# A hybrid-attention decoder trunk: the spread of the attention gate row behind the first output tile, and four adaLN sums six to three steps earlier

## The reference

```
mod = silu(c) @ w_ada[l] + b_ada[l]                 # six rows: sh1 sc1 gt1 sh2 sc2 gt2
h = x * (1 + sc1) + sh1
y = concat(rms_norm(window_attention(h)), rms_norm(sparse_attention(h))) @ w_o
x = layer_norm(ALPHA * x + (1 + gt1) * y)
h = x * (1 + sc2) + sh2
x = layer_norm(ALPHA * x + (1 + gt2) * swiglu(h))
```

## Time and profile before

| what | value |
|---|---|
| median of 3 runs | 1323.13 us (1321.76 to 1323.23) |
| the profiled execution | 1322.47 us, span 1320.7 us |
| TensorE matmul busy (PE) | 1256.3 us, 95% |
| VectorE busy (DVE) | 816.4 us, 62% |
| ScalarE busy (ACT) | 510.0 us, 39% |
| GpSimd busy (POOL) | 267.5 us, 20% |
| mean granted TensorE clock | 0.991 |

### The profile page before, as it was taken

The page is one execution under the profiler, slowest core; times in us unless marked ns, Lnnn a source line. Parts: engine busy times, 40 slices in busy tenths (PEclk is TensorE's granted clock), DMA queues, the critical chain, the costliest instruction groups (busy, mean ns, idle before and its releaser), DMA issues.

```text
span 1320.7 us, 18346 instructions
## 1 busy us (share of the span) xinstructions
PE 1256.3 (95%) x6368; PEld 1041.9 (79%) x6368; DVE 816.4 (62%) x1430; ACT 510.0 (39%) x1016; POOL 267.5 (20%) x258
## 2 busy tenths in 40 slices
PE   3999998999999999999999999899999999999996
PEld 3787776788888878888879687788888878888884
DVE  6779999656767765333675678955643345433337
ACT  3444557516333212222244556771543321222210
POOL 4116226800111100000006246671000000000001
PEclk9899999999999999999999999999999999999999
DMA  9563102231777735222424210012132233222211
GB/s 357 186 225 112 65 33 97 92 132 66 255 268 258 253 108 208 96 95 97 160 83 139 65 64 1 33 49 97 64 112 95 95 112 128 96 96 95 95 48 64
DMA packets 44849, 158.29 MB, mean 120 GB/s; under 512 B 5872, under 2 KB 5872, under 8 KB 44784
## 3 DMA queue, kind: packets, MB, share of 16 engines
q1 hardware_dynamic: 30528, 109.07, 24.0%
q0 software_dynamic: 12960, 47.19, 10.7%
q10 hardware_dynamic: 1296, 1.17, 0.3%
HBM read 155.31 MB, written 2.10 MB: 119 GB/s over the span
## 4 chain that ended last, share of the span: by engine, by line
PE 78%; DVE 13%; issue 4%; ACT 3%; POOL 1%; DMA 1%; DVEq 0%; ACTq 0%; POOLq 0%
PE bank L605 23%; PE bank L607 23%; PE bank L606 23%; DVE scores L1573 2%; PE bank L909 2%; PE bank L876 2%; DVE top L1565 2%; DVE w_lo L1423 2%; PE bank L855 1%; PE bank L887 1%; DVE pq L1612 1%; DVE ada_acc L1469 1%; PE bank L637 1%; ACT scratch L1180 1%; POOL w_raw L484 1%
## 5 line engine op out<-in xcount | busy, mean ns | idle before, releaser
L605 PE MATMUL bank<-hT_hi,w_hi 128*128 128x512 f32 (+1 forms) x768 | 286.3, 373 | 2.0 <-issue 1.5
L607 PE MATMUL bank<-hT_hi,w_lo 128*128 128x512 f32 (+1 forms) x768 | 285.3, 371 | 0.0
L606 PE MATMUL bank<-hT_lo,w_hi 128*128 128x512 f32 (+1 forms) x768 | 285.2, 371 | 0.0
L1829 DVE TENSOR_TENSOR w_lo<-w_raw,w_hi 128x1024 fp32r<-128x1024 f32 x88 | 107.8, 1225 | 149.8 <-ACT w_hi L1319 149.8
L1165 ACT ACTIVATE w_hi<-w_raw 128x1024 fp32r<-128x1024 f32 x96 | 100.5, 1062 | 208.7 <-PE bank L607 200.9
L605 PE MATMUL bank<-w_hi,hT_hi 128*128 128x512 f32 (+2 forms) x448 | 170.8, 381 | 4.1 <-ACT pq L1201 2.0
L605 PEld LDWEIGHTS bank<-hT_hi,w_hi 128*128 128x128 f32 x768 | 144.7, 188 | 28.0 <-issue 2.2
L606 PE MATMUL bank<-w_lo,hT_hi 128*128 128x512 f32 (+2 forms) x448 | 164.9, 368 | 0.0
L607 PE MATMUL bank<-w_hi,hT_lo 128*128 128x512 f32 (+2 forms) x448 | 164.7, 368 | 0.0
L607 PEld LDWEIGHTS bank<-hT_hi,w_lo 128*128 128x128 f32 x768 | 144.6, 188 | 25.3
L606 PEld LDWEIGHTS bank<-hT_lo,w_hi 128*128 128x128 f32 x768 | 144.7, 188 | 24.6
(11 more groups left out here) (172 smaller groups left out, 1878.2 us busy)
## 6 DMA issues: line engine op xcount, KB each, us to landing
w_raw<-in_weights SPq DMA_DIRECT2D x184, 512.0 KB, 3.5
ada_w<-in_w_ada POOLq DMA_DIRECT2D x80, 512.0 KB, 4.9
ada_w<-in_w_ada SPq DMA_DIRECT2D x4, 512.0 KB, 6.5
qT<-in_w_ada SPq DMA_DIRECT2D x4, 512.0 KB, 10.1
xs<-in_x SPq DMA_DIRECT2D x4, 512.0 KB, 15.6
g_row<-in_ln_row POOLq DMA_DIRECT2D x4, 512.0 KB, 5.5
b_row<-in_ln_row POOLq DMA_DIRECT2D x4, 512.0 KB, 6.8
trunk_out<-xs SPq DMA_DIRECT2D x8, 256.0 KB, 2.1
```

The source lines that it names most:

```text
L605: pe.matmul(dst, a_hi, b_hi, start=first, stop=False)
L606: pe.matmul(dst, a_hi, b_lo, start=False, stop=False)
L607: return pe.matmul(dst, a_lo, b_hi, start=False, stop=last)
L1829: nc.vector.tensor_tensor(w_lo[:, s, :], w_raw[:, s, :], w_hi[:, s, :].bitcast(F32), ALU.subtract).then_inc(lo_ready, 1)
```

## The change

In layer 0's attention the last four adaLN sums, and GpSimd's four fetches that go with them, move from steps 64, 65, 66, 67 to 58, 60, 62, 64. In both layers `spread_gate` moves behind `out_first` of tile 3, with its own waits. Nothing is added or removed.

```diff
-ASIDE_AT = (12, 18, 24, 30, 42, 46, 50, 54, 64, 65, 66, 67)
+ASIDE_AT = (12, 18, 24, 30, 42, 46, 50, 54, 58, 60, 62, 64)
...
                     if 0 <= i - LAG_V < 64:
                         head_values(l, (i - LAG_V) // 8, (i - LAG_V) % 8)
+                    if i - 64 - LAG_V in (0, 1):
+                        out_first(l, WO0_ORDER[i - 64 - LAG_V])
                     if i == 64 + LAG_V:
 
                         pe.wait_ge(masked, at_head(l, 7, 7))
                         spread_gate(l, 0, 4)
-                    if i - 64 - LAG_V in (0, 1):
-                        out_first(l, WO0_ORDER[i - 64 - LAG_V])
```

## The result

The change made the kernel slower by a quarter of a percent: 1324.62 us median of 20 runs, against 1322.10 for the kernel before, ratio 1.0023 with a 95% interval of 1.0013 to 1.0032, which is +3.0 us (+1.7 to +4.2); the means of the two sets are 3.0 us apart, the medians 2.5. The profiled execution took 1326.54 us, span 1324.8 us. Single runs spread over 6 us for either kernel, so a comparison of two whole traces says little about a change of this size: of the 4.1 us between the two spans, 2.25 had come about before the first moved instruction. I therefore read the stage from an anchor inside each trace: from the start of GpSimd's fourth low half (line 492, just ahead of the first difference) to TensorE's first product of the adaLN reduction behind tile 2 (line 629). I call this **the interval**.

The account below looks back on a forecast made before the run. Bound: GpSimd's late root for unit 6, delaying ScalarE's copies and TensorE's last products. Layer 0 +1.0, layer 1 +0.1 and clock +1.3 gave +2.4 us on the 1323.13 median: 1325.5 us, 8-in-10 range 1322.9 to 1327.6.

Parts of the forecast that it names:

- Fetches: GpSimd, layer 0: three fetches of 0.63 us each now stand ahead of unit 6's root, +1.9 us on the chain.
- Sums beside gains: Layer 0: GpSimd gains slowed by VectorE sums running beside them, +0.5 us, bounds 0 and 2.9.
- d = 2.4 us: Predicted delay of unit 6's root on GpSimd in layer 0: 1.9 for fetches plus 0.5 for sums beside gains.
- The removed wait: Layer 0, TensorE ahead of tile 3: its wait for the last adaLN sum before the spread goes, -1.4 us.
- The clock: TensorE, layer 0: idle growing to 3.2 us drops the next stretch to 1.2 GHz, +1.3 us, bounds 0 and 2.0.
- Layer 1: No sum is pending there; tile 3 now waits briefly for its low half, +0.1 us.
- Covers: VectorE's step 58 sum, late masks, late root ask and late gate take all stay hidden, price nothing.
- the line that I had drawn at 0.2%: Smallest difference from no change that a measurement of this kernel was said to tell: about 0.2%, 2.6 us.
- the clock holds: Rival, chance 0.25: neither TensorE stretch around the idle is empty enough to lower the clock; +1.1, 1324.2 us.
- GpSimd's delay is absorbed: Rival, chance 0.08: unit 6's root has hidden slack, so only the removed wait counts; 1321.8 us.
- the blocked case: Rival, chance 0.15: sums 60, 62 and 64 each take 0.9 to 1.0 us from a GpSimd gain half; 1327.8 us.
- low-clock stretch in layer 1: Rival, chance 0.10: the shift makes such a stretch come or go, 1.4 us either way; 1322.8 to 1326.9 us.

Follow-up runs that it names:

- fetches late: The change with GpSimd's four fetches put back at steps 64 to 67, sums left early; 1322.70 us, ratio 0.9994 to the kernel before.
- Short sum: The change with the sum of step 60 over only 64 of its 1024 columns; 1323.23 us, one run.
- spread only: The kernel before with only the spread moved, sums and fetches left at steps 64 to 67; 1321.87 us, ratio 0.9980.
- filled wait: The change with eight unused products in TensorE's idle ahead of the last head's transpose, layer 0; 1323.90 us, ratio 1.0002 to the kernel before.
- change, root first: The change with GpSimd's gains of steps 60 and 62 moved to 62 and 63, behind unit 6's root; 1322.29 us, ratio 0.9986 to before.

## Why the prediction was right, step by step

- **What bounds the stage.** Right: after 252.90 the root's delay passes through one to one. The root is 2.94 us later behind the anchor, TensorE's idle 2.95 us longer.
- **Fetches, +1.9 us.** Right. The three take 0.63, 0.58 and 0.58 us, and from each to the row behind it 0.68, 0.62 and 0.60, 1.9 in all; "fetches late" takes 2.2 us off the root, this and some of the contention, whose pattern shifts with it.
- **Sums beside gains, +0.5 us.** This is the term that was mis-sized. I had placed the gain of step 58 0.1 us ahead of sum 60 and so counted it as undisturbed. They started within 0.02 us of each other, the gain lost 1.08 us, and the second pair 0.1: +1.1 to 1.2 in all, inside the bounds of 0 and 2.9. "Short sum" shows that the sum was the cause. An order worked out to 0.1 us from the trace of before was not enough to choose between the two ends of the bound.
- **d = 2.4 us** was thereby 2.94, and layer 0 without the clock +1.5 instead of +1.0.
- **The removed wait, -1.4 us.** Nearly: "spread only" took 1.56 us off the interval.
- **The clock, +1.3 us.** Right: it fell, and cost 2.93 - 1.54 = 1.4 by the intervals (1.55 with the 1.56 of "spread only" in place of 1.4), 1.5 by the filled wait.
- **Layer 1, +0.1.** Right, 0.09. There the spread's move never gains, since no sum is pending.
- **Covers.** The sum of step 58, the late masks and ask, and the late take of the gate all stayed hidden, with 3.0 us left ahead of unit 7's low half in both layers.
- **Sum.** +2.4 forecast, +3.0 measured, by the intervals as by the timed runs. The 0.6 us is the contention term. The measured 0.23% lies just over the line that I had drawn at 0.2%, with an interval (0.13 to 0.32%) that reaches to both sides of it; but it excludes no change at all, so these runs told a change of 0.1% from none, and not only one of 0.2%. That the median of 1324.62 is only 0.9 us below the forecast of 1325.5 is partly luck: the forecast started from 1323.13, the median of three runs, and twenty runs gave 1322.10.
- **The rivals.** The case in which the clock holds and the one in which GpSimd's delay is absorbed did not occur. Of the blocked case about a third did: one sum of three, that of step 60, took 1.1 us from a gain, and this was a sign that I had named for it. By the condition that I gave there, slower from d = 2.7 with a fall of the clock, the measured d of 2.94 falls on its side. The low-clock stretch in layer 1 did move, from 785.5 to about 849.7 in the profiled executions, with the 1.18 us named above; what it is worth in the timed runs is not shown.

I had priced "the wait removed" against both parts of the change together. The runs show that either part removes it alone, so that the parts don't add: the spread's move is worth 1.56 us alone and nothing behind early sums.

## What to carry to other kernels

When a wait for a side task is to be removed, move the consumer behind independent work before moving the producer: the spread's move alone took 1.6 us off, while the producer's move brought a queue of another engine with it. Count, on every queue, each instruction that a shared step table moves ahead of a critical one, here three fetches of 0.6 us ahead of a root that others waited for. And look first at what stands ahead of a late small instruction: putting the root ahead of gains that nothing waited for yet gave 0.9 us for two changed table entries.

## What the runs showed of the hardware

- A gain of GpSimd, which reads SBUF, that starts while a VectorE sum with two inputs in SBUF runs ends late by nearly the rest of that sum: 1.08 us beside a sum that started at the same time and took 1.28, 0.48 beside one that had 0.6 us left. This agrees with the exclusive lock in the Trainium skill (SBUF — State Buffer, Who interferes with whom). A sum that starts inside a gain lost about 0.3 us (two took 2.86 instead of 2.54), less than that rule gives.
- Even an operation on one column is held up: GpSimd's root took 1.26 us instead of 0.58 when it started with 0.8 us of a sum left ("change, root first").
- An idle of 3.72 us of TensorE was followed by 3.4 us at 1.2 GHz, which cost 1.4 to 1.5 us; so were idles of 3.73 and 3.22 us in the same place, and idles of 1.51 and 1.52 us were not. Eight unused products of 3.6 us together kept 2.4 GHz.
